# Two transformer-like blocks on one core: the experts' gates scattered by indirect adds into a table in device memory, in place of a per-token gate stage

## What is computed

```python
def peer(xn, w_pq, sub_k1, sub_k2, expert_u, expert_v):
    q = (xn @ w_pq).reshape(B, S, PEER_HEADS, 2, PEER_HALF)
    s1 = einsum('bshd,hnd->bshn', q[..., 0, :], sub_k1)
    s2 = einsum('bshd,hnd->bshn', q[..., 1, :], sub_k2)
    v1, i1 = lax.top_k(s1, 16)
    v2, i2 = lax.top_k(s2, 16)
    cand = (v1[..., :, None] + v2[..., None, :]).reshape(B, S, PEER_HEADS, 256)
    vs, ci = lax.top_k(cand, 16)
    e1 = take_along_axis(i1, ci // 16, axis=-1)
    e2 = take_along_axis(i2, ci % 16, axis=-1)
    eidx = e1 * 128 + e2                      # an expert's number
    gates = softmax(vs, axis=-1)
    # per token t, over its 8 x 16 = 128 (expert, gate) pairs:
    act = gelu(einsum('tkd,td->tk', expert_u[eidx], xt))
    return einsum('tk,tkd->td', act * gates, expert_v[eidx])
```

## Time and profile before

| | us |
|---|---|
| median of 3 runs | 4177.9 (4169.02 to 4179.69) |
| profiled execution, device time | 4179.81 |
| its span in the trace | 4178.0 |
| PE busy | 3930.3, 94% of the span |
| DVE, ACT, POOL busy | 1773.7, 1709.3, 1409.3 |
| bytes moved | 636.19 MB, mean 152 GB/s |

### The profile page before, as it was taken

The page is one execution under the profiler, slowest core; times in us unless marked ns, Lnnn a source line. Parts: engine busy times, 40 slices in busy tenths (PEclk is TensorE's granted clock), DMA queues, the critical chain, the costliest instruction groups (busy, mean ns, idle before and its releaser), DMA issues. The chain is left out here.

```text
span 4178.0 us, 71583 instructions
## 1 busy us (share of the span) xinstructions
PE 3930.3 (94%) x23918; PEld 3540.3 (85%) x23918; DVE 1773.7 (42%) x3041; ACT 1709.3 (41%) x2889; POOL 1409.3 (34%) x1156
## 2 busy tenths in 40 slices
PE   7999999999899999979888998999997799999999
PEld 6888868889899997868468998999996688888879
DVE  4654412113666663344343397222227733333344
ACT  1121121004555554544224454554444355555544
POOL 0001000004444444433013444444445444444434
PEclk9999989999999999989868999999996599999999
DMA  4443424445455555534214554555551055555544
GB/s 159 137 140 119 131 91 132 153 154 174 143 181 181 183 183 182 192 108 149 71 61 156 169 171 139 184 182 181 181 183 65 0 186 193 193 192 194 192 146 161
DMA packets 173004, 636.19 MB, mean 152 GB/s; under 512 B 19232, under 2 KB 19360, under 8 KB 172400
## 3 DMA queue, kind: packets, MB, share of 16 engines
q1 hardware_dynamic: 172512, 630.40, 46.2%
q0 software_dynamic: 400, 4.52, 0.3%
HBM read 630.65 MB, written 4.19 MB: 152 GB/s over the span
## 5 line engine op out<-in xcount | busy, mean ns | idle before, releaser
L401 POOL TENSOR_TENSOR wlo<-ring,whi 128x512 fp32r<-128x512 f32 x938 | 1258.0, 1342 | 1615.2 <-ACT whi L393 1614.5
L393 ACT ACTIVATE whi<-ring 128x512 fp32r<-128x512 f32 x1876 | 1177.8, 633 | 1264.6 <-PE ps L509 802.3
L507 PE MATMUL ps<-xhi,whi 128*128 128x256 f32 x4752 | 1360.5, 286 | 74.3 <-POOL xlo L423 24.7
L401 DVE TENSOR_TENSOR wlo<-ring,whi 128x512 fp32r<-128x512 f32 x938 | 707.7, 757 | 1553.2 <-ACT whi L393 1549.0
L508 PE MATMUL ps<-xlo,whi 128*128 128x256 f32 x4752 | 1355.4, 285 | 0.0
L509 PE MATMUL ps<-xhi,wlo 128*128 128x256 f32 x4752 | 1355.0, 285 | 0.0
L507 PEld LDWEIGHTS ps<-xhi,whi 128*128 128x128 f32 x4752 | 923.2, 194 | 79.9 <-issue 50.6
L508 PEld LDWEIGHTS ps<-xlo,whi 128*128 128x128 f32 x4752 | 923.4, 194 | 0.2
L509 PEld LDWEIGHTS ps<-xhi,wlo 128*128 128x128 f32 x4752 | 922.9, 194 | 0.0
L496 PE MATMUL ps<-hn,ring 128*128 128x256 f32 x3040 | 670.2, 382 | 6.9 <-DVE hn L1047 6.0
L496 PEld LDWEIGHTS ps<-hn,ring 128*128 128x128 f32 x3040 | 581.1, 192 | 89.6 <-issue 9.9
(11 more groups left out here) (189 smaller groups left out, 2289.7 us busy)
## 6 DMA issues: line engine op xcount, KB each, us to landing
ring<-stream SPq DMA_DIRECT2D x1190, 512.0 KB, 3.8
res<-xT SPq DMA_DIRECT2D x1, 2048.0 KB, 9.8
outT<-res POOLq DMA_DIRECT2D x1, 2048.0 KB, 7.8
parked<-outT POOLq DMA_DIRECT2D x1, 2048.0 KB, 10.3
outT<-res SPq DMA_DIRECT2D x4, 512.0 KB, 5.6
mixcon<-mixc SPq DMA_DIRECT2D x1, 1664.0 KB, 16.0
par<-params SPq DMA_DIRECT2D x1, 287.0 KB, 2.7
parked<-pT POOLq DMA_DIRECT2D x1, 256.0 KB, 10.7
```

What stands on the lines that cost most here:

```text
L393: act.activation(quarters(whi, g), quarters(ring[:, n % SLOTS, :], g), ACT.Copy).then_inc(w_hi, 1)
L401: eng.tensor_tensor(quarters(wlo, g), quarters(ring[:, n % SLOTS, :], g), quarters(whi, g).bitcast(F32), ALU.subtract).then_inc(done, 1)
L507: pe.matmul(out, whi[:, b], hi, start=start, stop=False, **kw)
```

## The change

A table `gates` of 128 x 128 x 256 floats (16.8 MB) in device memory takes the place of the per-token products. It has one float for every expert and token.

- POOL sets it to zero during **up**: one memset of `zeros`, and then, after every fourth of 64 panels, a DMA of 1 MB.
- DVE works out, after the expert numbers, the place of each (token, expert) pair in the table: four more operations.
- POOL makes its rests up to eu panel 32 (`OWN`). From panel 33 on DVE makes all four quarters (`rests_both`), and POOL issues 256 indirect DMAs, each of which adds 128 floats (one per partition, that is one per token) at 128 places. A head's 32 have all to land before the next head's are issued, since two heads may name one expert.
- When all have landed POOL loads the first two groups of gate tiles (4 tiles, 512 KB each) into `gate_ring`; the further 30 groups are loaded during **ev**, between its rests.
- DVE multiplies each tile of A by its tile of gates one panel ahead of its use (`gate`), and ACT waits for that (`gated`).
- The transposes after panel 64, `token`, `rows`, `weigh` and both `two` are gone. PE waits for A's last tile and goes on with **ev**.

```diff
+        gates = nc.dram_tensor("gates", (NK * P * T, 1), F32, kind="Internal").ap()
+        gate_rows = gates.rearrange("(p n) o -> p (n o)", p=P)
+        gate_tiles = gates.rearrange("(e p t) o -> p e (t o)", p=P, t=T)
...
+        def rests_both(dve, n, i=None, per=0):
+            for g in range(4):
+                dve.wait_ge(w_hi, turn(i, 4 * per, 4 * split_index(n) + g + 1))
+                dve.tensor_tensor(quarters(wlo, g), quarters(ring[:, n % SLOTS, :], g), quarters(whi, g).bitcast(F32),
+                                  ALU.subtract).then_inc((w_lo_pool, w_lo_dve)[g % 2], 1)
...
@@ PE @@
-            split_loop(PANELS["eu"], OUT["eu"], NK // 2)
-            pe.wait_ge(S["pk_et"], 1)
...
-            split_loop(PANELS["eu"] + NK // 2, OUT["eu"] + NK // 2, NK // 2)
-            for t in range(16):
-                token(t)
...
-            pe.wait_ge(S["tok_ev"], T // 4)
+            split_loop(PANELS["eu"], OUT["eu"], NK)
+            pe.wait_ge(evac_done, OUT["pg"])
             accumulate_all(PANELS["ev"], NK, FT)
...
@@ DVE @@
+            dve.wait_ge(res_parked, 16)
+            at = cdf[0]
+            L(stt(at, etm[:, 0:T], float(NK), etm[:, T:2 * T], ALU.mult, ALU.add))
+            L(ts(at, at, float(T), con[:, CC["lane"]:CC["lane"] + 1], ALU.mult, ALU.add))
+            L(ts(at[:, P:T], at[:, P:T], float(P), None, ALU.add))
+            L(dve.tensor_copy(place, at))
             dve.wait_ge(S["pk_e"], 1)
...
+            rests_loop(dve, eu, PANELS["eu"] + OWN + 1 - eu)
+            dve.wait_ge(w_lo_pool, 2 * split_index(PANELS["eu"] + OWN + 1))
+            with dve.Fori(0, (NK - OWN) // 4) as i:
+                for j in range(4):
+                    rests_both(dve, PANELS["eu"] + OWN + 1 + j, i, 4)
+            dve.wait_ge(evac_done, OUT["pg"])
...
+            def gate(k, i=None):
+                if k % 4 == 0:
+                    dve.wait_ge(gates_in[k // 4 % 2], turn(i, 16, 16 * (k // 8 + 1)))
+                c = A[:, k * T:(k + 1) * T] if i is None else A[:, bass.ds(i * (8 * T) + k * T, T)]
+                tell("gated", tt(c, c, gate_ring[k // 4 % 2][:, k % 4 * T:(k % 4 + 1) * T], ALU.mult))
...
@@ POOL @@
-            rests_loop(pool, PANELS["up"] + 1, 2 * FT + FT)
+            pool.memset(zeros, 0.0).then_inc(S["zero_set"], 1)
+            pool.wait_ge(S["zero_set"], 1)
+            with pool.Fori(0, 16) as i:
+                for j in range(4):
+                    rests(pool, PANELS["up"] + 1 + j, i, 4)
+                pool.dma_start(gate_rows[:, bass.ds(i * D, D)], zeros).then_inc(zeroed, 16)
+            rests_loop(pool, PANELS["up"] + 65, 3 * FT - 64)
+            pool.wait_ge(zeroed, 256)
...
-            rests_loop(pool, PANELS["eu"], NK + 1)
+            rests_loop(pool, PANELS["eu"], OWN + 1)
+            pool.wait_ge(S["pk_et"], 1)
+            for h in range(PH):
+                if h:
+                    pool.wait_ge(scattered, 16 * 2 * TOPK * h)
+                for k in range(TOPK):
+                    for b in range(2):
+                        c = b * P + h * TOPK + k
+                        pool.indirect_dma_start(gates, bass.IndirectOffsetOnAxis(ap=place[:, c:c + 1], axis=0), weight[:, c:c + 1], None,
+                                                compute_op=ALU.add).then_inc(scattered, 16)
+            pool.wait_ge(scattered, 16 * 2 * TOPK * PH)
+            for q in range(2):
+                gate_load(q)
             pool.wait_ge(panel_done, PANELS["ev"])
...
-            rests_loop(pool, PANELS["ev"] + 1, NK - 1)
+            with pool.Fori(0, NK // 8 - 1) as i:
+                for q in range(2):
+                    for j in range(4):
+                        rests(pool, PANELS["ev"] + 1 + 4 * q + j, i, 8)
+                    pool.wait_ge(S["gated"], turn(i, 8, 4 * q + 4))
+                    gate_load(q + 2, i)
```

More of the change, by code:

```diff
@@ L55 @@
 GATES_HEAD = 3
+OWN = 32
 PANELS = {}
@@ L127 @@
 _n = 0
-for _name, _k in (("ident", P), ("ones", P), ("iota", P), ("invfreq", 1), ("perm", 64)):
+for _name, _k in (("ident", P), ("ones", P), ("iota", P), ("invfreq", 1), ("perm", 64), ("lane", 1)):
     CC[_name] = _n
@@ L332, in two_blocks_kernel @@
         TAIL = NK * T
[L333 to L336, removed]
+        place = area3(TAIL, T).bitcast(U32)
+        weight = area3(TAIL + T, T)
+        gate_ring = [area3(TAIL + (2 + 4 * k) * T, 4 * T) for k in range(2)]
+        zeros = area2(29312, 2048)
         rows2 = area3(8192, 2 * D)
@@ L351, in two_blocks_kernel @@
         res_parked, res_back = sem("res_parked"), sem("res_back")
+        zeroed, scattered = sem("zeroed"), sem("scattered")
+        gates_in = [sem(f"gates_in{k}") for k in range(2)]
         panel_done = sem("panel_done")
@@ L367, in two_blocks_kernel @@
             "at_qn", "at_rot", "at_rotc", "at_done", "at_s", "at_mx", "at_e", "at_p", "at_t", "at_tc", "at_o", "at_oc",
-            "pk_s", "pk_sc", "pk_g", "pk_e", "pk_et", "pk_t", "pk_tc", "oh1_done", "oh2_done", "oh2_turn", "oh2_act", "oh2_sq", "tok_mm", "tok_ev",
+            "pk_s", "pk_sc", "pk_g", "pk_e", "pk_et", "zero_set", "gated",
             "pp_out", "pp_ev", "out_ready")}
@@ L969, in _ @@
             mm.then_inc(panel_done, 1)
-            split_loop(PANELS["eu"], OUT["eu"], NK // 2)
-            pe.wait_ge(S["pk_et"], 1)
[L974 to L977, removed]
-            split_loop(PANELS["eu"] + NK // 2, OUT["eu"] + NK // 2, NK // 2)
[L979 to L995, removed]
-            for t in range(16):
-                token(t)
-            with pe.Fori(0, T // 16 - 1) as i:
-                for t in range(16, 32):
-                    token(t, i)
-            pe.wait_ge(S["tok_ev"], T // 4)
+            split_loop(PANELS["eu"], OUT["eu"], NK)
+            pe.wait_ge(evac_done, OUT["pg"])
             accumulate_all(PANELS["ev"], NK, FT)
@@ L1376, in _, with tile_rest @@
             tile_c = Count(dve, tile_lo)
-            def tile_rest(k, src, before, i=None):
-                dve.wait_ge(tile_hi, turn(i, 4, before + k + 1))
-                c = src[:, k * T:(k + 1) * T] if i is None else src[:, bass.ds(i * (4 * T) + k * T, T)]
+            def tile_rest(k, src, before, i=None, per=4):
+                dve.wait_ge(tile_hi, turn(i, per, before + k + 1))
+                c = src[:, k * T:(k + 1) * T] if i is None else src[:, bass.ds(i * (per * T) + k * T, T)]
                 tile_c.mark(tt(tlo[k % 2], c, thi[k % 2].bitcast(F32), ALU.subtract))
@@ L1571, in _ @@
             L(dve.reciprocal(gsum, gsum))
[L1572 to L1577, removed]
-            for k in range(2):
-                L(dve.tensor_copy(et[:, k * T:(k + 1) * T], ps[:, 4 + k, 0:T]))
-            tell("pk_tc", dve.tensor_copy(et[:, 2 * T:3 * T], ps[:, 6, 0:T]))
@@ L1581, in _ @@
[L1581 to L1615, removed]
@@ L1616, in _ @@
-            dve.wait_ge(S["tok_mm"], T)
-            weigh(T // 4 - 1)
-            accumulation_rests(PANELS["ev"], NK, A, FT)
+            tell("pk_et", tt(weight.rearrange("p (h k) -> p h k", k=16), c3, gsum.unsqueeze(2).to_broadcast([P, 16, 16]), ALU.mult))
+            rests_loop(dve, eu, PANELS["eu"] + OWN + 1 - eu)
[3 more added lines that the diff above has]
+                    rests_both(dve, PANELS["eu"] + OWN + 1 + j, i, 4)
@@ new lines, in _ @@
+            dve.wait_ge(evac_done, OUT["pg"])
+            N["gated"] = Count(dve, S["gated"])
+            def gate(k, i=None):
[3 more added lines that the diff above has]
+                tell("gated", tt(c, c, gate_ring[k // 4 % 2][:, k % 4 * T:(k % 4 + 1) * T], ALU.mult))
+            for k in range(2):
+                gate(k)
@@ new lines, in _ @@
+            tile_rest(0, A, FT)
+            with dve.Fori(0, NK // 8 - 1) as i:
+                tile_c.enter(i, 8)
+                N["gated"].enter(i, 8)
+                for k in range(1, 9):
+                    gate(k + 1, i)
+                    tile_rest(k, A, FT, i, 8)
+                    rests(dve, PANELS["ev"] + k, i, 8)
+                tile_c.leave(NK // 8 - 1)
+                N["gated"].leave(NK // 8 - 1)
+            for k in range(NK - 7, NK):
+                if k + 1 < NK:
+                    gate(k + 1)
+                tile_rest(k, A, FT)
+                rests(dve, PANELS["ev"] + k)
@@ L1702, in x_high_norm, with accumulation_high @@
                     x_high(act, name, q, nx())
-            def accumulation_high(n, count, src, before):
+            def accumulation_high(n, count, src, before, gated=None):
                 def tile(k, i=None):
                     act.wait_ge(panel_done, turn(i, 4, n + k - 1))
+                    if gated is not None:
+                        act.wait_ge(gated, turn(i, 4, k + 1))
                     c = src[:, k * T:(k + 1) * T] if i is None else src[:, bass.ds(i * (4 * T) + k * T, T)]
@@ L1989, in _ @@
             experts(24, 40)
-            act.wait_ge(S["pk_tc"], 1)
             experts(64, 64)
[L1994 to L2019, removed]
```

(32 more changed lines are left out.)

## The result

The changed kernel takes 3999.85 us, median of 4 runs (3989.86 to 4008.06), against 4173.71 us of the kernel before in 4 runs of the same comparison. The ratio is 0.9579, 95% interval 0.9562 to 0.9596: 4.2% faster. The prediction was 4000.0 us.

The account below looks back on a forecast made before the run. PE was taken to bound eu and ev, with the gate stage a gap between them. 4179.8 - 185.1 + 2.4 - 2.7 + 1.6 + 1 + 3 = 4000.0 us, adds costing 0; range 3988 to 4186 us.

Parts of the forecast that it names:

- The gate stage removed: Between eu and ev: the gap in PE's timeline goes away, -185.1 us.
- The seam: Between eu and ev: a short chain to A's first gated tile leaves PE a gap, +2.4 us.
- Clock: At ev's start: no fall of PE's clock after the short gap, so the former slow start goes, -2.7 us.
- Places: After the expert numbers: four more DVE operations, charged whole because PE waits for DVE there, +1.6 us.
- Memset: On POOL before its first rest of up: zeroing, hidden at best, 5.2 us at worst, taken as +1 us.
- Stores of zeros: During up: 16 stores of 1 MB fit POOL's idle stretches, cost 0, upper bound 19 us.
- The parked rows: At ev's start: their loading makes two or three stream halves late, +3 us.
- The adds: Under eu from panel 32 on: 256 indirect adds at 1.3 us each, done 180 us early, cost 0.
- my threshold: Under eu: 519 us left for 256 adds, 2.03 us each; above it every 0.1 us costs 25.6 us.
- POOL gives way to DVE: Adds under eu: issues stand still during DVE's rests, 1.3 becomes 2.5 us, kernel 4062 us; partly covered, chance 0.17 for both mechanisms.
- The DMA engines: Adds under eu: elements held 179 ns each behind the stream, kernel 4137 us; partly covered, chance 0.17 for both mechanisms.
- One by one: POOL's queue after panel 32: each add waits for its landing, 3.8 us, kernel 4454 us; chance 0.20.

Follow-up runs that it names:

- e2: The changed kernel with only the adds of the first four of eight heads (128 of 256): 3987.81 us, ratio 0.9553 to the kernel before.
- e1: The changed kernel with POOL keeping its rests up to panel 64, so the adds begin later: 4160.95 us, ratio 0.9964 to the kernel before.
- e0: The changed kernel run again, unaltered, beside the other runs: 3993.41 us, ratio 0.9557 to the kernel before.
- e6: The changed kernel with POOL's rests handed over at panel 28 and the parked rows loaded after ev's panels: 3987.78 us, ratio 0.9564 to the kernel before.
- e3: The changed kernel with POOL keeping its rests up to panel 124, so nearly all adds run after the keys: 4474.45 us, one execution.
- e5: The changed kernel with adds begun at panel 64, each over 64 partitions instead of 128: 4109.21 us, ratio 0.9856 to the kernel before.
- e4: The changed kernel with adds begun at panel 64 and replaced by indirect writes: 4026.11 us, ratio 0.9653 to the kernel before.

## Why the prediction was right, and where it was not

The mechanism, a gap of 185 us replaced by a seam because the adds fit under the keys, is shown: by the trace after, by e2 (halving the adds changes nothing) and by e1 (delaying them by 185 us costs 167). The sum, term by term:

- *The gate stage removed*, -185.1: as read.
- *The seam*, +2.4: measured 2.86 us.
- *Clock*, -2.7, "I expect no fall": wrong in the step. Behind the gap of 2.86 us PE ran six matmuls at full clock, and then the spacing rose from 0.23 to 0.43 us for eight matmuls, from 3161.2 to 3164.6 us: the granted clock fell to its lower level (1.2 of 2.4 GHz; the stretch from 3162 to 3167 has 0.74). In the profiles of e0, e2 and e6, with gaps of 2.86 to 2.87 us, the first or second matmul already has the wide spacing, and again it lasts for seven or eight. From ev's start to the end of the span it is 840.4 us before and 839.2 after, so the term is -1.2. The spacings alone give -2.7 + 8 x 0.20 = -1.1.
- *Places*, +1.6: the four operations with their handing over took 1.44 us on DVE. The keys end 4.32 us later than before; 2.0 us of that were there already where up begins, ahead of the zeros, the places and the adds. What of the other 2.3 us is theirs and what scatter, one execution can't tell.
- *Memset*, +1: it took 1.82 us, and the first rest of up still waited 0.94 us for ACT behind it, so it cost nothing. *Stores of zeros*, 0: right, 0.57 us an issue, no gap of PE.
- *The parked rows*, +3: nothing. The DMA engines were 88 to 90% busy for some us, but PE has no gap in ev's first panels, and e6 without this collision is no faster.
- *The adds*, 1.3 us each and a cost of 0: the cost was right, the size wrong, and this is the step that came near to failing the prediction. I doubled the plain issue and reckoned with nothing between two. Measured are 1.62 us on average, mostly 0.30 us between, and the six pauses of 23.2 us together. With the seven drains between the adds taken off that is (537.1 - 25.5) / 256 = 2.00 us against my threshold of 2.03. "180 early" was 3.6 us early, and 0.4 in e0. The threshold itself was good: window 553.5 us (3158.2 - 2604.7) against 554, drains 30.3 us against 8 x 3.8. Only the first load took 8.0 us and not 5, which brings it to (553.5 - 30.3 - 8.0) / 256 = 2.01.

The memset and the parked rows, 4 us charged for nothing, were made good by what was charged too low: the clock by 1.5 us, the seam by 0.5, and the keys' later end, 4.3 us where 1.6 stood for the places. That the sum hits within 1 us is luck. That the adds cost nothing at all is luck as well: the guess of 1.3 us was off by 0.7, and the room left was 0.01 us an add. The range was earned by the threshold: its upper end allows adds of up to 2.7 us.

The rivals. *POOL gives way to DVE:* with DVE's rests and the stream beside it the issue is 5% longer (1620 against 1545 ns), not 92%. The row with 3.30 us was a subtraction on POOL beside a product on DVE, and the issue of an add didn't stretch like it. *The DMA engines:* in 200 us of the adds' stretch the queue of the adds shows

```profile
q1 hardware_dynamic: 9991, 36.36, 58.5%
q0 software_dynamic: 13489, 0.05, 17.6%
```

which is 0.176 x 16 x 200 us / 13489 = 42 ns a packet, not 179; the stream's landing grew from 3.8 to 4.5 us in this stretch, of 8.7 that it may take. *One by one:* for 242 of the 255 following adds the issue begins 0.30 us after the last one ends. Seven wait for a drain, and six for the pauses above, which are as long as a landing: 3.0 to 4.8 us in the changed kernel, 1.8 to 2.0 in e3.

The Trainium skill gives a DMA of this path a fixed cost of about 2.0 us, most of it the receipt of the write ("DMA: Bandwidth & Descriptors", "Anatomy of one DMA — SWDGE (gpsimd) path"). In e3, with nothing else running, POOL waits 1.77 us after the last issue, which is near it; under load the trace shows up to 4.80. The Trainium skill's rule of about 102 cycles a small read ("GPSIMD Engine Reference", "Performance pitfalls for Q7 kernels") doesn't hold for these addresses: e5 shows 2.2 ns an element, and the whole issue for 128 takes 1.55 us.

## What to carry to other kernels

When work is moved under a long stage, work out how much each of its instructions may cost before the cover is gone, and look at that number rather than at the cost you guess: here 2.03 us were allowed, 2.00 were used, and the guess was 1.3. In this kernel the many small DMAs issued by POOL are priced by the instruction, its fixed issue and the pause behind it, far more than by the elements or by what else runs (load made the chain 9% longer, 537.1 against 494.4 us). Start such a chain as early as its inputs allow, even where it makes no time today, since past the margin nearly every us of delay is a us of the kernel (e1: 161 us of 185).

## What the runs showed of the hardware

- POOL's issue of a DMA: plain 0.55 to 0.58 us for 128 rows, 0.76 us for 512 pieces of 1 KB, indirect write of 128 floats 1.13 us beside the stream and 0.96 us without it (e4), indirect add of 128 floats 1.55 us, of 64 floats 1.41 us (e5); 0.30 us between two.
- POOL pauses for about as long as a landing though the program doesn't ask for it: with adds over 128 partitions before the 61st, 114th, 121st, 181st, 227th and 241st, with adds over 64 partitions (e5) and with writes (e4) before the 114th and 227th alone; 3.0 to 4.8 us in the changed kernel, 1.8 to 2.0 us without load (e3). What it waits for isn't shown.
- A gap of 2.9 us in a stream of matmuls without gaps was followed by some 3.4 us at half clock in all four profiles that were read for it (the changed kernel, e0, e2, e6), beginning 1.4 us after the gap's end in the first and at once, or one matmul later, in the others.
